# A top-k search by halving: six tiles instead of four searched in the first part, and the second part's order taken from one clock

## What is computed

```python
h = rmsnorm(x, g_pre)
u_a, gate_a, q, k, v, qi, ki, wi, gate_b = split(h @ w_in)          # 2600 columns
dots  = einsum('bqhd,bkd->bqhk', qi, ki)                            # 8 index heads x 32
score = einsum('bqh,bqhk->bqk', wi, relu(dots)) * INDEX_SCALE
score = where(key_chunk <= query_chunk, score, -inf)
_, sel = top_k(score, 256)                                          # per query row
p = softmax(q . k[sel] * scale + rel_bias[bucket(sel - pos)])       # 8 heads x 64, 2 kv heads
y_b = p . v[sel]
mixed = concat(pool_mixer(u_a) * silu(gate_a), y_b * silu(gate_b))
out = x + rmsnorm(mixed @ w_out, g_post)                            # also k, v, ki are returned
```

## Time and profile before

| | |
|---|---|
| median of 3 runs | 1634.06 us (1633.37 to 1636.78) |
| profiled execution, its own time | 1636.42 us |
| span in its trace, first to last instruction | 1634.4 us, mean granted PE clock 0.969 |
| first part, to 764.9 us | 47% of the span |
| busy share of the span | PE 92%, DVE 70%, ACT 54%, POOL 29% |

### The profile page before, as it was taken

The page is one execution under the profiler, slowest core; times in us unless marked ns, Lnnn a source line. Parts: engine busy times, 40 slices in busy tenths (PEclk is TensorE's granted clock), DMA queues, the critical chain, the costliest instruction groups (busy, mean ns, idle before and its releaser), DMA issues.

```text
span 1634.4 us, 17094 instructions
## 1 busy us (share of the span) xinstructions
PE 1504.7 (92%) x4935; PEld 849.2 (52%) x4935; DVE 1142.1 (70%) x2753; ACT 889.4 (54%) x1684; POOL 467.6 (29%) x387
## 2 busy tenths in 40 slices
PE   7999899999999999988888888999989998899996
PEld 4555555555555887756444444444444444454552
DVE  5412577769998556665347999999999989885312
ACT  3112333333334445552289999998889896633331
POOL 0111211121111323211333444443433433332241
PEclk9999999999999999988799999999999999999999
DMA  9322222231111110146622222221220101202111
GB/s 368 67 59 49 74 55 64 56 100 48 61 47 58 60 47 35 45 135 173 223 63 58 74 53 75 79 60 48 57 84 26 47 27 32 58 14 80 33 39 45
DMA packets 89990, 117.56 MB, mean 72 GB/s; under 512 B 16957, under 2 KB 63613, under 8 KB 89514
## 3 DMA queue, kind: packets, MB, share of 16 engines
q1 hardware_dynamic: 88666, 112.55, 22.2%
q10 hardware_dynamic: 1232, 3.93, 2.2%
HBM read 71.87 MB, written 43.54 MB: 71 GB/s over the span
## 4 chain that ended last, share of the span: by engine, by line
PE 26%; DVE 13%; ACT 7%; issue 5%; POOL 2%; POOLq 0%; ACTq 0%; DVEq 0%
PE wide L1703 9%; PE wide L1688 8%; DVE above L344 4%; ACT act_junk L1579 3%; PE bank L1663 2%; PE bank L1664 2%; PE bank L1665 2%; DVE max_junk L1768 2%; PE bank L1636 2%; POOL E L1538 1%; ACT E L1613 1%; ACT act_search L1587 1%; DVE S L379 1%; PE wide L1636 1%; DVE osb L1823 1%
## 5 line engine op out<-in xcount | busy, mean ns | idle before, releaser
L931 PE MATMUL bank<-hT,home 128*128 128x512 f32 (+2 forms) x1280 | 487.3, 517 | 5.1 <-DVE sga L1146 2.4
L1538 POOL TENSOR_TENSOR E<-E,home 128x512 f32<-128x512 f32 (+1 forms) x174 | 240.3, 1384 | 453.4 <-ACT E L1613 453.2
L931 PEld LDWEIGHTS bank<-hT,home 128*128 128x128 f32 x1280 | 235.7, 191 | 165.1 <-issue 142.8
L1688 PE MATMUL wide<-E,home 128*128 128x512 f32 x544 | 286.0, 608 | 15.1 <-POOL E L1538 15.1
L1613 ACT ACTIVATE E<-bank 128x512 f32<-128x512 f32 (+1 forms) x290 | 165.2, 570 | 198.6 <-PE bank L1665 179.2
L907 ACT ACTIVATE relu<-wide 128x1024 f32<-128x1024 f32 (+7 forms) x192 | 153.9, 802 | 213.6 <-PE wide L949 161.4
L1184 DVE SCALAR_TENSOR_TENSOR S<-relu,wi,S 128x1024 f32<-128x1024 f32 (+7 forms) x168 | 173.7, 1034 | 103.7 <-ACT relu L907 96.2
L1768 DVE CUSTOM_DVE_ANT_0 max_junk<-bank,mask 128x512 bf16<-128x512 f32 (+3 forms) x235 | 138.1, 607 | 81.6 <-PE bank L1636 61.8
L1703 PE MATMUL wide<-home 128*128 128x512 f32 x272 | 145.7, 627 | 35.7 <-ACT osb L1605 35.6
L1579 ACT ACTIVATE act_junk<-S,minus_cand 128x1152 uint8<-128x1152 f32 (+5 forms) x105 | 155.4, 1480 | 1.5
L949 PE MATMUL wide<-kiT,qiT 96*128 96x512 f32 (+3 forms) x304 | 139.4, 527 | 6.4 <-ACT relu L907 6.4
(11 more groups left out here) (216 smaller groups left out, 2231.0 us busy)
## 6 DMA issues: line engine op xcount, KB each, us to landing
xs<-x_prompt SPq DMA_DIRECT2D x16, 512.0 KB, 4.2
home<-w_in SPq DMA_DIRECT2D x16, 512.0 KB, 14.2
xr<-x_prompt SPq DMA_DIRECT2D x16, 512.0 KB, 4.2
y_prompt<-osb SPq DMA_DIRECT2D x16, 512.0 KB, 2.8
first_q<-q_high_scratch SPq DMA_DIRECT2D x24, 256.0 KB, 4.7
s_scratch<-S SPq DMA_DIRECT2D x11, 512.0 KB, 2.7
gb<-gb_scratch SPq DMA_DIRECT2D x17, 256.0 KB, 5.1
home<-ma_scratch SPq DMA_DIRECT2D x17, 256.0 KB, 5.1
```

The source lines that it names most:

```text
L931: mm = pe.matmul(out, stationary(c), moving(c), start=(c == 0), stop=(c == DC - 1))
L1538: pool.tensor_tensor(E[:, k % 4, :, 0:n], E[:, k % 4, :, 0:n], EB[:, kv * GRP:(kv + 1) * GRP, off:off + n], ALU.mult)\
L1688: pe.matmul(wide[0][:, kv * 512:kv * 512 + GRP * n].rearrange("p (j n) -> p j n", j=GRP), values[:, kt, kv:kv + 2, :].rearrange("p a d -> ...
```

## The change

In the first part, tiles 2 to 7 are searched instead of 2 to 5. Rounds 0 to 15 of each (steps SK, with the scaling SN ahead of them) are done by ACT, rounds 16 to 25 (SP) and `choose` (SC, cut into four parts) by DVE. Each round is one step of its own, and rounds are spread evenly between the score pieces of a projection step. How many are taken is set by a cost for each and a budget of 4.4 for each projection step (2.42 for the steps of the fourth and fifth block, TM excepted). In the second part tiles 8 to 16 are searched; every engine's order, POOL's and SP's too, is sorted on one axis of planned times (`start`, at 3.5 a key tile and 14 for an output product), and the search of a tile is laid over this axis by `search_bounds`, no longer bound to a step. `choose` is cut into four parts there too. Masks of searched tiles now go from `B.reach` through DRAM into `mask` (SP's MS and ML). The junk output of the norm's square becomes uint8, and one wait of DVE on its own chain is added before the unseen keys are overwritten.

```diff
+ROUND_TRIP = 14.0
+SEARCH_ROOM = 4.4
-EARLY = range(TOPK // P, 6)
-SEARCH_PIECES = [(r, min(r + 4, ALL_ROUNDS)) for r in range(0, ALL_ROUNDS, 4)]
+EARLY = range(TOPK // P, 8)
+CHOICES = 4
...
+def early_search(t):
+    n = key_tiles(t)
+    return ([(("SN", t), 0.14 * n)] + [(("SK", t, r), 0.143 * n + 0.78) for r in range(ZOOM_AT)]
+            + [(("SP", t, r), 0.155 * n + 0.45) for r in range(ZOOM_AT, ALL_ROUNDS)]
+            + [(("SC", t, part), 0.3 * n + 0.3) for part in range(CHOICES)])
...
-    def seek():
-
-        if seeking:
-            steps.append(seeking.pop(0))
-            if steps[-1][0] == "SM" and seeking:
-                steps.append(seeking.pop(0))
+    def seek(pieces, room):
+
+        taken = []
+        while seeking and room > 0 and seeking[0][0][0] not in ("SL", "SM"):
+            item, cost = seeking.pop(0)
+            taken.append(item)
+            room -= cost
+        if not taken:
+            while seeking and seeking[0][0][0] in ("SL", "SM"):
+                steps.append(seeking.pop(0)[0])
+        marks = sorted([((i + 0.5) / len(pieces), 0, x) for i, x in enumerate(pieces)]
+                       + [((i + 0.4) / len(taken), 1, x) for i, x in enumerate(taken)], key=lambda m: m[:2])
+        steps.extend(x for *_, x in marks)
...
+            room = (SEARCH_ROOM if nt == 4 else 0.55 * SEARCH_ROOM)
             if t:
-                seek()
-                project(("TM", t), 1 + sum(taking))
+                project(("TM", t), 1 + sum(taking), SEARCH_ROOM)
...
-                if step[0] != "Q":
-                    seek()
-                project(step, sum(taking[j:]) if taking[j] else 0)
+                project(step, sum(taking[j:]) if taking[j] else 0, room)
...
+                    elif s[0] == "SK":
+                        _, t, r = s
+                        w = key_tiles(t) * P
+                        act.wait_ge(early_halved, halved_by(t, r, 0))
+                        act.wait_ge(ss_done, norms)
...
+                            act.activation(junk[:, 0:w], Se[:, 0:w], ACT.Sign, bias=minus_cand[:], accum_out=tally[:])\
+                               .then_inc(early_halved, 1)
...
+                        act.activation(side[:], tally[:], ACT.Sign, bias=enough[:, t - EARLY[0]:t - EARLY[0] + 1])\
+                           .then_inc(early_halved, 1)
...
+    STEPS = range(-1, NT + 3)
+    start = {-1: -6.0}
+    for t in STEPS:
+        tiles = key_tiles(t) if 0 <= t < NPT else 4 if t == ST else 0
+        start[t + 1] = start[t] + 3.5 * tiles + (14.0 if 0 <= t - 2 < NT else 0.5) + (5.5 if t == -1 else 0.0)
+
+    def when(t, share):
+        return start[t] + share * (start[t + 1] - start[t])
+
+    def search_bounds():
+        tiles = list(range(FIRST, NT))
+        size = [0.0]
+        for u in tiles:
+            size.append(size[-1] + key_tiles(u) + 3)
+        size.append(size[-1] + key_tiles(tiles[-1]) + 3)
+        limit = {i + 2: when(u - 1, maxima_from(u)) - ROUND_TRIP for i, u in enumerate(tiles)}
+        bounds = [start[0]]
+        while len(bounds) < len(size):
+            at = len(bounds) - 1
+            ends = [j for j in limit if j > at]
+            pace = {j: (limit[j] - bounds[at]) / (size[j] - size[at]) for j in ends}
+            tight = min(ends, key=pace.get)
+            for j in range(at + 1, tight + 1):
+                bounds.append(bounds[at] + pace[tight] * (size[j] - size[at]))
+        return {u: tuple(bounds[i:i + 3]) for i, u in enumerate(tiles)}
...
+        for u, (_, a, b) in bounds.items():
+            tiles = key_tiles(u)
+            costs = [(("R", u, r), 0.155 * tiles + 0.4) for r in range(ZOOM_AT, ALL_ROUNDS)]
+            costs += [(("C", u, part), tiles * (0.25, 0.28, 0.2, 0.3)[part] + 0.3) for part in range(CHOICES)]
...
+        for u, (a, b, _) in bounds.items():
             pieces = [("N", u)]
             for r in range(ZOOM_AT):
                 pieces += [("K", u, r), ("T", u, r)]
...
+        for u, (_, _, b) in bounds.items():
+            series.append(([("MS", u)], b + 1.5, 0.0))
+            series.append(([("ML", u)], max(b + 5.0, when(u - 2, 0.0) + 0.5), 0.0))
...
+                    elif kind == "MS":
+                        t = at[0]
+                        n = key_tiles(t) * P
+                        sp.wait_ge(mask_ready, t - FIRST + 1)
+                        sp.dma_start(m_dram[t, :, 0:n], B.reach[:, 0:n]).then_inc(mask_out, 16)
```

More of the change, by code:

```diff
@@ L110, in spread, with project @@
             steps.append(pending.pop(0))
-    def project(step, left):
+    def project(step, left, room=0.0):
         k = -(-len(pending) // left) if left > 0 else 0
@@ L210, in phase1_steps @@
     settle()
-    while seeking:
-        seek()
+    steps.extend(item for item, _ in seeking)
     return steps, inside
@@ L355, in halve, with choose @@
     return n
-def choose(dve, done, n, B, i, s):
+def choose(dve, done, n, B, s, part):
     def link(ins):
@@ L1620, in _ @@
                         while waiting:
                             take_sums(*waiting.pop(0))
+                    else:
+                        t, kv, kt = at
+                        k = fl[t, kv, kt]
+                        act.wait_ge(fl_full, k + 1)
+                        if k >= 4:
+                            act.wait_ge(pv_step, k - 3)
+                        n = queries(t)
+                        act.activation(E[:, k % 4, :, 0:n],
+                                       banks[2 + k % 2][:, 0:GRP * n].rearrange("p (j n) -> p j n", j=GRP), ACT.Exp).then_inc(fl_free, 1)
+                        while waiting and last_fl(*waiting[0]) <= k - 2:
+                            take_sums(*waiting.pop(0))
+                        if kt == key_tiles(t) - 1:
+                            waiting.append((t, kv))
```

515 lines of the change are left out of this document (282 added, 233 removed).

## The result

The changed kernel takes **1644.95 us** (median of 4 runs, 1641.27 to 1645.88) against 1633.93 of the kernel before on the same chip (1633.37 to 1636.78): ratio 1.0059, 95% interval 1.0043 to 1.0076. It is 0.6% slower, clear of the interval; 1607 us had been forecast, in a range of 1580 to 1641. The profiled execution took 1641.27 us, the lowest of the four, so its span of 1639.4 is only 5.0 above that of before where the medians are 11 apart.

The account below looks back on a forecast made before the run. PE was taken to bound the first part and, after the change, nearly all of the second. 793 + 88 + 579 + 147 gave a span of 1607; +2.0 and -2.4 made 1606.5, forecast 1607 us, range 1580 to 1641.

Parts of the forecast that it names:

- the 552 by the terms for PE: Second part's middle, turn of tile 4's maxima to tile 15's: PE's work alone would need 552 us.
- the new sum: Same middle after the change: largest engine load of each step adds up to 553 us, against 606 before.
- Rival A: First part hides the searches (+12), second part takes 557: -66 us, 1568; with half of it 1585; chance 0.18.
- First part, +28 forecast: Added searches lengthen the short steps of tiles 13 to 16 by 28 us, between +17 and +38; first part 793.
- The steps up to tile 12: First part up to 538.3 us: rounds only move from DVE to ACT, so 0, between -5 and +6 us.
- rival B: First part, blocks 4 and 5: waits lower PE's clock from 0.98 to 0.80, adding 33 us; whole 1639 or 1663; chance 0.11.
- Start and end, 88 and 147 forecast: Second part's start falls by 3 us from 91.0, between -6 and +3; its end stays, 5 us against if DVE is late.
- The masks through DRAM, put at 0: Store and load of nine masks take some 8 us each where 14 are planned, so the wait is covered.
- Rival C: Searches stay on the path as DRAM masks lengthen each lateness; middle stretch 603 or more, whole 1630, no change; chance 0.11.
- POOL: Cutting choose counted as no gain: the running sum stays whole, so PE's 15.7 us of waits for POOL would stay.
- The middle of the second part, 579 forecast: Turn of tile 4's maxima to tile 15's: 553 plus 26 us makes 579, a gain of 53; bounds 557 and 603.
- The coupling: Second part's middle: time queues lose to each other above summed largest loads, kept at 26 us (4%); bounds 4 us and 9%.

Follow-up runs that it names:

- e_mix: Changed kernel with tiles 2 to 6 searched in the first part, tiles 2 to 5 by VectorE alone and only tile 6 shared with ScalarE; 1624.65 us, ratio 0.9955.
- n_s2: Changed kernel with both engines' second-part search rounds counting over the first 128 keys only; 1605.93 us (one run), middle stretch 577.7.
- e_old2: Changed kernel's first part with the second part in the orders of the kernel before; 1655.62 us, ratio 1.0138.
- a_pn: Changed kernel with the post-norm later: VectorE at 0.9 of a step, GpSimd's addition at 0.97, SyncE's store in the next step; 1615.99 us, ratio 0.9891.
- e27: Changed kernel with tiles 2 to 6 instead of 2 to 7 searched in the first part; 1630.26 us, ratio 0.9981.
- e_pn: e_mix with the post-norm at 0.9 of a step on VectorE, and GpSimd's and SyncE's following work shifted too; 1608.54 us, ratio 0.9852.
- b_pn: Kernel before with VectorE's post-norm at 0.88 of a step, ahead of choose, and GpSimd's addition at the step's end; 1670.31 us, ratio 1.0223.

## Why the prediction was wrong, point by point

The median came 38 us above the forecast. By the prediction's own stages 29 of them are the middle of the second part, 3 the first part, 1 the start less 1 of the end, and 6 that the profiled execution lies below the median, where I had put the median 0.4 under the span.

**What bounds.** Right: with less search work in the second part and the same work for PE, the middle became 23.4 us shorter, and with the rounds' passes narrow it takes 577.7 us, 26 above the 552 by the terms for PE. In the first part PE had been the bound, and added search work made it longer. Worked out again, the printed terms give 549 for PE alone and 551.5 for the new sum, in place of 552 and 553; nothing here turns on that. Rival A's second number doesn't come out either: half of its -66 us gives 1601, not 1585.

**First part, +28 forecast, +30.9 measured: right**, with its place: tiles 13 to 16 "some 180" long, 185.7 measured; DVE 145 and ACT 125 busy forecast, 134.6 and 118.2 measured. Two parts of its working were off and small. The steps up to tile 12 were put at 0 with +6 as the bound; they took 2.9 us more (538.3 to 541.2), and 3.6 to 5.8 more in the five other kernels with this first part. e_mix puts such a loss on ScalarE's rounds of tiles 2 to 5. And rival B's mechanism is in the 29.5: the clock fell, but to 0.94 and not to 0.80, for 7.7 us. The rule that I set against the change, of the Trainium skill (Perfetto Trace Analysis, Identifying the Most-Contended Engine), that the most contended engine be relieved first, would give no gain here, and the runs agree: +30.9 us. It does not tell that tile 6 breaks even and tile 7 loses 11.

**Start and end, 88 and 147 forecast, 89.3 and 146.0 measured.** Right. The masks through DRAM, put at 0, cost near 0: VectorE's maxima waited 3.0 us for one of them, once. Rival C had the right outcome for the stretch, 603 or more, and half of its mechanism: the searches did stay on PE's path (30.6 us of the stretch by n_s2), but not through late masks.

**POOL.** I counted nothing for `choose` cut in parts, since the running sum stays whole, so PE's 13.6 us of waits for GpSimd in this stretch would have stayed. They fell to 1.7, and in e_old2, where `choose` is cut but its parts stand together, they are 13.4: it is the spreading that helps, not the cut. The Trainium skill (SBUF - State Buffer, Who interferes with whom) says that an instruction of VectorE with two SBUF inputs contends with one of GpSimd that reads SBUF. The trace agrees, and the contention is still there after the change: in the changed kernel's middle stretch one bias product of GpSimd beside a running sum takes 4.37 us, and another with no running sum beside it 1.28 (GpSimd, VectorE, GpSimd).

```profile
1239.67 1.28 POOL L1676 TENSOR_TENSOR E<-E,home 128x512 f32<-128x512 f32 x1 [16.22 <-ACT E L1753]
1243.79 3.89 DVE L389 TENSOR_TENSOR_SCAN S<-reach,above 128x1792 f32<-128x1792 bf16 x1
1244.38 4.37 POOL L1676 TENSOR_TENSOR E<-E,home 128x512 f32<-128x512 f32 x1 [3.43 <-ACT E L1753]
```

What went is PE's wait for it. My step from "GpSimd is held up" to "PE waits as before" was the wrong one; what lets PE go on was not tried by a run of its own.

**The middle of the second part, 579 forecast, 608.3 measured: this step failed**, and in it one term. The coupling, "I add the same 26 us", came out as 55, over my bound of 9%. The runs say where most of the other 29 go: with the post-norm out of the maxima (a_pn) the stretch is 583.1 and the coupling 30, near the 26 that I had taken. So 25.2 us are the place of the post-norm. I had read the coupling as a share of time that goes with the layout, from 4 to 9%, and the waits of the output bank as its known part. Waits of the kernel before in its stretch:

```profile
POOL osb L1501 <- DVE osb L1823: 29.9, 8, 4.6
...
PE wide L1703 <- ACT osb L1605: 25.5, 15, 4.2
...
PE wide L1688 <- POOL E L1538: 13.6, 7, 3.1
...
PE wide L1636 <- DVE mxp L1768: 12.1, 9, 2.3
PE bank L1636 <- DVE mxp L1768: 8.1, 11, 2.1
```

The output bank's fell (25.5 to 14.4 us), where I had said that they would stay. PE's waits for maxima grew, 20.2 to 26.3, where I had said that they would shrink, and these come from what stands beside the maxima on VectorE. The whole time above PE's 552 is then, in the changed kernel, 43.5 us of idle PE, 26.3 of it for maxima, and 13 of busy time above the terms. I had the whole new order of VectorE in hand, `P` at 0.5 of a step and the parts of `choose` wherever the clock puts them, and summed it by step instead of reading it as a queue with two spare banks in front of it. GpSimd's wait of 29.9 us for the post-norm stood in the trace of before as well, and I took no row of it.

**Tile 7.** The sums give 564 with tile 7 in the second part and 553 without, a gain of 11. With the post-norm amid the maxima it gave 2.5 (e27 to the changed kernel), with the late post-norm 14.2 (e_pn to a_pn). Its price in the first part is 14.5, so with the fault mended it breaks even and doesn't pay. What is left of e_pn's lead over a_pn (7.4 us by the medians, 4.2 by the profiled spans) is about what the sharing of tiles 2 to 5 costs.

**What stays open.** Whether the new layout loses more in the meetings themselves or in the bias products behind GpSimd's wait was split in e_mix (8.8 and 4.6), not in the changed kernel. That the 30.6 us of n_s2 and the 25.2 of a_pn overlap is likely, since together they would leave 552, the bare sum of PE's terms, but no run has both; so either of the two, the searches' passes or the post-norm between them, can be called the cause of the same microseconds. And no run moved ScalarE's rounds away from the emptying of the output bank, for which PE still waits 13.8 us in a_pn.

## What to carry to other kernels

When several engines are within some 10% of each other, the sum of the largest load of each step is only a floor. Here 26 to 55 us lay above it, and nearly half of the 55 hung on which long items stood next to each other in the queue that feeds the bounding engine, with few buffers between the two. List for each short-buffered handover (here the maxima, three banks) the longest run of other work between two of its items, and move the removable item out before moving work between stages. Check first that the place it goes to is empty: the same move made one order 25 us faster and the other 36 slower.

## What the runs showed of the hardware

A short wait costs PE more than itself: after one of 3.7 us two value products took 1.91 instead of 1.02 us, and in b_pn a wait of 5.0 us leaves the next 10 us at a mean clock of 0.66, where 1.00 is 2.4 GHz and 0.5 is 1.2 GHz.

The scaling of the mask, one bf16 operand in and out, takes very different times. The one at 1262.45 above ran beside GpSimd's addition (L1642, from 1260.56 to 1264.61); this one ran with GpSimd idle:

```profile
1348.78 0.66 DVE L1886 TENSOR_SCALAR reach<-reach 128x1920 bf16<-128x1920 bf16 x1
```

Four times as long for fewer columns: 2.65 us at 1792 (fence above) against 0.66 at 1920. It is not one odd pair. The second part of the changed kernel has nine such scalings: the six that run beside GpSimd for 1.1 us or more take 1.42 to 2.65 us, the three that don't 0.46 to 0.69. In e_old2 the same nine all run with GpSimd idle and take 0.46 to 0.69. In sum they are 13.0 us against 5.1: a price of the spread order that nothing in the prediction had. It is not what the late post-norm gave back, for in a_pn they still take 12.2. The Trainium skill (SBUF - State Buffer, Who interferes with whom) says that VectorE's two-port modes contend with GpSimd and that `tensor_scalar` can enter them; the trace agrees. It is one more reason to keep such a step away from maxima that PE waits for.
